# Expert weights streamed through a six-slot ring, moved in half matrices instead of whole ones

## The reference, cut to what matters

```python
N_EXPERTS, EXPERT_HIDDEN, D = 32, 512, 1024     # w_gate, w_up: [32, 1024, 512]; w_down: [32, 512, 1024]

def expert_block(args):
    xblk, e = args
    hid = jax.nn.silu(xblk @ w_gate[e]) * (xblk @ w_up[e])
    return hid @ w_down[e]
```

## Time and profile before

| | us |
|---|---|
| median of 3 runs (2041.07 to 2042.13) | 2041.3 |
| the profiled execution | 2040.8 |
| its span in the profile | 2039.0 |

### The profile page before, as it was taken

How to read it: one execution, slowest core, us unless ns; L and a number is a source line. 1 busy time by engine, 2 the same in 40 slices (tenths; PEclk the granted TensorE clock), 3 DMA queues, 4 the chain that set the end, 5 groups by cost and what they waited for, 6 DMA issues and landing times.

```text
span 2039.0 us, 25122 instructions
## 1 busy us (share of the span) xinstructions
PE 1973.0 (97%) x10310; PEld 1335.8 (66%) x10310; DVE 582.1 (29%) x1351; ACT 424.1 (21%) x961; POOL 12.9 (1%) x34
## 2 busy tenths in 40 slices
PE   8999999999999999998999999999998999999998
PEld 7798888957988888666455445445885455545544
DVE  3277450422555603422111011102233011101111
ACT  2440000322301101322221222122102222122212
POOL 1000000000001000000000000000000000000000
PEclk9998999989999999989999999999999999999999
DMA  9645576432357753213999999999544999999995
GB/s 334 199 170 218 236 305 247 166 111 84 137 233 285 306 220 132 83 42 123 400 429 429 427 429 429 428 429 428 208 148 157 400 430 427 429 428 428 428 429 226
DMA packets 51580, 591.24 MB, mean 290 GB/s; under 512 B 6305, under 2 KB 14761, under 8 KB 15794
## 3 DMA queue, kind: packets, MB, share of 16 engines
q1 hardware_dynamic: 51218, 588.09, 71.0%
q10 hardware_dynamic: 288, 2.10, 0.3%
HBM read 584.69 MB, written 1.05 MB: 287 GB/s over the span
## 4 chain that ended last, share of the span: by engine, by line
PE 70%; DMA 24%; DVE 4%; issue 1%; SPq 0%; ACT 0%; DVEq 0%
PE ps L436 24%; DMA ring<-in_w_up 22%; PE ps L1077 15%; PE ps L668 7%; PE ps L1167 4%; PE ps L1059 2%; PE ps L1065 2%; PE ps L711 2%; PE ps L495 2%; DVE work L1690 1%; DMA ring<-in_w_ada 1%; PE ps L583 1%; PE ps L462 1%; PE ps L511 1%; PE ps L526 1%
## 5 line engine op out<-in xcount | busy, mean ns | idle before, releaser
L1077 PE MATMUL ps<-ring,work 128*64 128x512 f32 x2048 | 450.3, 593 | 12.7 <-DMA ring<-in_w_up 12.2
L436 PE MATMUL ps<-h,ring 128*128 128x256 f32 x2064 | 457.1, 383 | 3.0 <-DVE h L1952 2.2
L436 PEld LDWEIGHTS ps<-h,ring 128*128 128x128 f32 x2064 | 394.0, 192 | 58.8 <-issue 4.0
L1077 PEld LDWEIGHTS ps<-ring,work 128*64 128x64 f32 x2048 | 151.2, 137 | 305.1 <-issue 290.4
L1349 ACT ACTIVATE work<-ps 128x512 f32<-128x512 f32 (+1 forms) x186 | 95.7, 519 | 715.0 <-PE ps L436 302.0
L1167 PE MATMUL ps<-ring,work 128*64 128x512 f32 x1024 | 226.8, 595 | 1.6 <-DVE work L2150 1.6
L1349 ACT ACTIVATE work<-ps,ada,scale_g 128x128 f32<-128x128 f32 x256 | 96.2, 456 | 411.3 <-PE ps L1059 411.3
L2141 DVE TENSOR_TENSOR work<-ps,work 128x512 f32<-128x512 f32 x32 | 22.1, 692 | 551.9 <-ACT work L1349 551.9
L1167 PEld LDWEIGHTS ps<-ring,work 128*64 128x64 f32 x1024 | 70.6, 137 | 133.6 <-issue 128.0
L668 PE MATMUL ps<-work,ring 128*128 128x256 f32 (+1 forms) x704 | 150.0, 376 | 3.9 <-DVE work L1867 3.9
L668 PEld LDWEIGHTS ps<-work,ring 128*128 128x128 f32 x704 | 131.3, 192 | 22.0 <-DVE work L1867 4.6
(11 more groups left out here) (295 smaller groups left out, 1282.2 us busy)
## 6 DMA issues: line engine op xcount, KB each, us to landing
ring<-in_w_gate SPq DMA_DIRECT2D x64, 2048.0 KB, 15.0
ring<-in_w_up SPq DMA_DIRECT2D x64, 2048.0 KB, 17.3
ring<-in_w_down SPq DMA_DIRECT2D x64, 2048.0 KB, 12.2
ring<-in_w_ada SPq DMA_DIRECT2D x24, 2048.0 KB, 8.5
ring<-in_w_ff_gate SPq DMA_DIRECT2D x10, 2048.0 KB, 14.8
ring<-in_w_ff_up SPq DMA_DIRECT2D x10, 2048.0 KB, 12.8
ring<-in_w_ff_down SPq DMA_DIRECT2D x8, 2048.0 KB, 10.9
ring<-in_ml_w_in SPq DMA_DIRECT2D x6, 2048.0 KB, 10.7
```

The lines of the kernel that those rows point to most:

```text
L436: last = mm(ps[:, b, 0:T], w[:, k, m * P:(m + 1) * P], rhs[:, k, :], start=(k == 0), stop=(k == nk - 1))
L1077: last = mm(ps[e * CAP:(e + 1) * CAP, j, :], xg[:, k, e * CAP:(e + 1) * CAP], w[e][:, k, :], start=(k == 0), stop=(k == KT - 1))
```

## The change

Each expert matrix is loaded by two DMAs of 1 MiB, each the first or the second half of every partition's row. In `gathered_tokens` the halves have signals of their own: `gate_half` and `up_half` after step k = 3, beside `gate_full` and `up_full`; for down the existing `half_done` and `down_done`. SP waits for a half's signal and loads that half of both experts of the next pair. PE still waits for both halves of both matrices before it begins with a kind. The down matrix is stored with its column half outermost, so that half a row is what one value of c reads. The wait values go from 16 to 32 per expert load (`landed`). The branch for crowded experts (`all_tokens`) waits as before and loads two halves each time. To have semaphores for the new signals, some that are never needed apart are merged (`lru_decay` and `lru_root` into `lru_powers`, `f_abs` and `gate_m` into `gate_args`, `z_sq` and `z_root` into `z_stats`, `all_squares` into `row_full`); each waiter waits for the same instructions as before.

```diff
@@ PE, gathered_tokens and its helpers
-                    gate_step(k, [matrices(first, e)[2][0] for e in range(2)])
+                    last = gate_step(k, [matrices(first, e)[2][0] for e in range(2)], last_k=KT // 2 - 1)
+                last.then_inc(e_["gate_half"], 1)
...
-                            pe.wait_ge(slot_loaded[slots[j]], 16 * i + loads[j])
+                            pe.wait_ge(slot_loaded[slots[j]], 32 * i + loads[j])
...
                             last = gate_step(k, [pair_of[e][2][j] for e in range(2)], j)
+                            if k == KT // 2 - 1:
+                                last.then_inc(e_["up_half" if j else "gate_half"], 1)
                         last.then_inc(e_[done], 1)
...
-                                          pair_of[e][2][2][:, k, c * 512:(c + 1) * 512],
+                                          pair_of[e][2][2][:, c, k, :],
@@ SP, load_experts
-                order = [(0, 0), (0, 1), (1, 0), (1, 1), (2, 0), (2, 1)]
+                order = [(w, e) for w in range(3) for e in range(2)]
+
+                def load_half(w, e, part, expert):
+
+                    slot = (first + 2 * w + e) % RING
+                    at = slice(part * SLOT // 2, (part + 1) * SLOT // 2)
+                    sp.dma_start(ring[:, slot, at], weights[w][l, expert][:, at]).then_inc(slot_loaded[slot], 16)
+
                 for j, (w, e) in enumerate(order):
-                    n = first + j
-                    sp.wait_ge(*released[n - RING])
-                    sp.dma_start(ring[:, n % RING, :], weights[w][l, e]).then_inc(slot_loaded[n % RING], 16)
+                    sp.wait_ge(*released[first + j - RING])
+                    for part in range(2):
+                        load_half(w, e, part, e)
...
-                    with sp.Fori(0, NEXP // 2 - 1) as i:
-                        for j, (w, e) in enumerate(order):
-
-                            s_, per, at = done(w, e)
-                            sp.wait_ge(s_, per * i + at)
-                            slot = (first + j) % RING
-                            sp.dma_start(ring[:, slot, :], weights[w][l, 2 * i + (2 + e)]).then_inc(
-                                slot_loaded[slot], 16)
...
+                def pairs_of_gathered_tokens():
+
+                    freed = (("gate_half", "gate_full"), ("up_half", "up_full"), ("half_done", "down_done"))
+                    with sp.Fori(0, NEXP // 2 - 1) as i:
+                        for w in range(3):
+                            for part in range(2):
+                                sp.wait_ge(e_[freed[w][part]], i + 1)
+                                for e in range(2):
+                                    load_half(w, e, part, 2 * i + (2 + e))
+                    next_layer(lambda w, e: (e_[freed[w][1]], 1, 1))
@@ layout of the down matrices in DRAM
-    w = g["w_down_2"].reshape(2, NEXP, HTL, P, D)
-    arrays["w_down"] = np.ascontiguousarray(w.transpose(0, 1, 3, 2, 4)).reshape(2, NEXP, P, SLOT)
+    w = g["w_down_2"].reshape(2, NEXP, HTL, P, 2, D // 2)
+    arrays["w_down"] = np.ascontiguousarray(w.transpose(0, 1, 3, 4, 2, 5)).reshape(2, NEXP, P, SLOT)
```

More of the change, by code:

```diff
@@ L368, in build, with landed @@
         seam_rows = (HTL + 2 * HTL, KT - 1 + 2, KT - 3 + 2 * 3)
+        def landed(n):
+            experts = lambda m: any(0 <= m - first < 3 * NEXP for first in moe_first)
+            return sum(32 if experts(m) else 16 for m in range(n % RING, n + 1, RING))
         def conditions(l, c):
@@ L415, in next_chunk @@
                     state["chunk"] += 1
-                pe.wait_ge(slot_loaded[n % RING], 16 * (n // RING + 1))
+                pe.wait_ge(slot_loaded[n % RING], landed(n))
                 _, nk, cols = chunks[n]
@@ L1071, in matrices, with gate_step @@
                 slots = [j % RING for j in n]
-                return slots, [16 * (j // RING + 1) for j in n], [
-                    ring[:, slots[j], :].rearrange("p (k c) -> p k c", k=KT if j < 2 else HTL) for j in range(3)]
-            def gate_step(k, w, j=0):
+                return slots, [landed(j) for j in n], [
+                    ring[:, slots[0], :].rearrange("p (k c) -> p k c", k=KT),
+                    ring[:, slots[1], :].rearrange("p (k c) -> p k c", k=KT),
+                    ring[:, slots[2], :].rearrange("p (h k c) -> p h k c", h=2, k=HTL)]
+            def gate_step(k, w, j=0, last_k=KT - 1):
                 for e in range(2):
                     last = mm(ps[e * CAP:(e + 1) * CAP, j, :], xg[:, k, e * CAP:(e + 1) * CAP], w[e][:, k, :],
-                              start=(k == 0), stop=(k == KT - 1))
+                              start=(k == 0), stop=(k == last_k), skip_group_check=True)
                 return last
@@ L1161, in down @@
                     for slots, loads, _ in pair_of:
-                        pe.wait_ge(slot_loaded[slots[2]], 16 * i + loads[2])
+                        pe.wait_ge(slot_loaded[slots[2]], 32 * i + loads[2])
                     for c in range(2):
@@ L1278, in rest, with pairs_of_all_tokens, done @@
                             put(n)
+                def pairs_of_all_tokens():
+                    def done(w, e):
+                        return ((e_["gate_full"], 8, 4 * e + 4), (e_["up_full"], 8, 4 * e + 4), (e_["down_done"], 2, e + 1))[w]
+                    with sp.Fori(0, NEXP // 2 - 1) as i:
+                        for w, e in order:
+                            s_, per, at = done(w, e)
+                            sp.wait_ge(s_, per * i + at)
+                            for part in range(2):
+                                load_half(w, e, part, 2 * i + (2 + e))
+                    next_layer(done)
+                def pairs_of_gathered_tokens():
+                    freed = (("gate_half", "gate_full"), ("up_half", "up_full"), ("half_done", "down_done"))
+                    with sp.Fori(0, NEXP // 2 - 1) as i:
+                        for w in range(3):
+                            for part in range(2):
+                                sp.wait_ge(e_[freed[w][part]], i + 1)
+                                for e in range(2):
+                                    load_half(w, e, part, 2 * i + (2 + e))
+                    next_layer(lambda w, e: (e_[freed[w][1]], 1, 1))
                 with sp.If(most > CAP):
-                    rest(lambda w, e: ((e_["gate_full"], 8, 4 * e + 4), (e_["up_full"], 8, 4 * e + 4),
-                                       (e_["down_done"], 2, e + 1))[w])
+                    pairs_of_all_tokens()
                 with sp.Else():
-                    rest(lambda w, e: (e_[("gate_full", "up_full", "down_done")[w]], 1, 1))
+                    pairs_of_gathered_tokens()
             load(1)
@@ L1432, in _ @@
             for j in range(HTL):
-                turn.give(A(rate[:, j, :], th[:, j, :], ACT.Exp, scale=lamt[:, 24 + j:25 + j]), S["lru_decay"])
-            turn.own(S["lru_decay"])
+                turn.give(A(rate[:, j, :], th[:, j, :], ACT.Exp, scale=lamt[:, 24 + j:25 + j]), S["lru_powers"])
+            turn.own(S["lru_powers"])
             for j in range(HTL):
@@ L1511, in _ @@
             value_out(0, 0)
-            turn.take(S["f_abs"])
+            turn.take(S["gate_args"])
             turn.give(A(ghead[:, 2, :], ghead[:, 2, :], ACT.Exp, scale=-1.0), achain)
@@ L1517, in _ @@
             value_out(1, 0)
-            turn.take(S["gate_m"])
+            turn.take(S["gate_args"])
             turn.give(A(ghead[:, 3, :], ghead[:, 3, :], ACT.Exp, scale=-1.0), S["gate_expm"])
@@ L1795, in _ @@
             step(V.tensor_tensor(bx[:], bx[:], xr[:], ALU.mult))
-            turn.take(S["lru_decay"], HTL)
-            turn.take(S["lru_root"])
+            turn.take(S["lru_powers"], HTL)
+            turn.take(S["lru_powers"])
             step(stt(den_a, rate, 1.0, den_a, ALU.add, ALU.mult))
@@ L1826, in ada_make @@
                 if half == 0:
-                    dve.wait_ge(slot_loaded[n % RING], 16 * (n // RING + 1))
+                    dve.wait_ge(slot_loaded[n % RING], landed(n))
                 ws = range(conditions(l, c))
@@ L2000, in _ @@
                 if i == 3:
-                    turn.take(S["z_root"])
-                    turn.take(S["z_sq"], TT)
+                    turn.take(S["z_stats"])
+                    turn.take(S["z_stats"], TT)
                     step(V.reciprocal(small[:, 8:10], small[:, 6:8]))
```

38 lines of the change are left out of this document (19 added, 19 removed).

## The result

| | before | after |
|---|---|---|
| median of 20 runs each, us | 2041.17 (2037.93 to 2046.56) | 2046.51 (2040.01 to 2053.76) |
| ratio of after to before, 95% interval | | 1.0023 (1.0014 to 1.0033) |
| span of the profiled execution, us | 2039.0 | 2041.3 |
| its time, us | 2040.8 | 2043.1 |

The change made the kernel 5.3 us slower by the medians, 0.26% (the ratio in the table is 1.0023). In the profiles much of the difference between two executions arises ahead of the expert stages: the first gate product comes at 951.96 us in after, at 954.41 before, and anywhere from 951.50 to 958.00 in the other kernels of this document, which ahead of it differ at most in pair 0's loads and the merged semaphores.

The account below looks back on a forecast made before the run. The DMA queue's rate was taken to bound the late expert pairs. Per layer, -3.51 (early down) + 6.25 (rows) + 0.39 (DMAs) = +3.13 us; two layers +6.3, so the median becomes 2047.6 us, range 2036.5 to 2053.5.

Parts of the forecast that it names:

- What bounds the kernel: Mixture layers, late pairs: paced by what the DMA queue can move, 428.6 GB/s, not by when a slot comes free.
- The knot's spacing: Repeating waits from the fifth pair (in_w_up DMA, PE's up products, next DMA): starts 29.36 us apart, forecast to become 29.84.
- the rival of depth: Late pairs: a longer queue makes the engines move more, so PE sets the pace; about -17 us, 2024.8; chance 0.03.
- The price of a row: Expert loads: each extra row costs an engine 9.3 ns; 672 rows more make 6.25 us a layer (3.96 to 8.47).
- The price of twice the DMAs: Expert loads: signals of 84 more DMAs to the load that counts, 0 to 0.78 us a layer, 0.39 taken.
- The early half of down: Pair 1's first down half is issued 3.51 us earlier, into an empty queue: -3.51 us a layer, -7.0 in all.
- one sign named for being wrong: Queue ahead of pair 1's down: an idle stretch as long as now would show the prediction wrong.
- Gate and up halves bring nothing: Other 14 pairs: gate and up halves released earlier only lengthen a queue that is never empty: 0.
- The rest at 0: PE's matmuls, down's new column order, signals added to matmuls and merged semaphores: 0; nothing waits for anything new.
- the pair where PE begins to wait: Mixture layers: PE begins to wait at the sixth or seventh pair instead of the fifth.
- Sum of a layer: Each mixture layer: -3.51 + 6.25 + 0.39 = +3.13 us; two layers +6.3.
- The rival of free rows: Expert loads: rows of 8 KiB cost nothing more, leaving -7.0 us: 2034.3, or up to 2037.2; chance 0.13.

Follow-up runs that it names:

- the late and the early kernel: Late: the changed kernel, each half loaded only when the kernel before would have loaded the whole matrix, +12.2 us against before; early: the changed kernel itself, +5.3 us.
- The run with pair 1 alone: Kernel before, with only pair 1's down matrices loaded in halves, the first behind half_done; all other pairs whole: -1.4 us, ratio 0.9982 to 1.0001.

## Why the prediction was right

The forecast was 2047.6, the median is 2046.5, inside the range, and in the direction forecast. By its steps:

- *What bounds the kernel.* Right. The knot's spacing is a pair's bytes at the queue's rate: every kernel with shorter rows throughout moved it (29.53, 29.69, 29.82, 30.72), and the three that load later pairs whole and only issued some loads earlier kept it (29.36, 29.37, 29.36). With more loads waiting in it the queue was not faster (29.82 in after, 29.83 with the same halves released late), so the rival of depth falls as well.
- *The price of a row,* 9.3 ns with ends at 5.9 and 12.6, taken from 1 KiB rows. Measured 9.5 ns at 8 KiB and 9.4 at 4 KiB. The four readings from the narrow chunks scattered by a factor of two, and their mean lay well; the spread of the range was honest and the mean partly luck. The estimate from the 408.7 GB/s that the Trainium skill gives ("DMA: Bandwidth & Descriptors", section "iDMA fabric — 4 AXI ports for 8 engines, asymmetric across TPBs"), 9.9 ns, is borne out too: the run with 4 KiB rows moved 410 GB/s.
- *The price of twice the DMAs,* 0.39 us a layer: put too high. Twelve DMAs and six with the same rows have spacings 0.01 and 0.02 us apart, 0.1 to 0.3 us a layer, and after, with twelve, has the spacing of six.
- *The early half of down,* -3.51 us: -3.57 and -3.52 between the late and the early kernel. Right in size and in time (978.88 is 26.9 us behind pair 0's gate; the 981.4 forecast was 27.0 behind its own). But one sign named for being wrong, an idle stretch ahead of down as long as now, came nearly true: 2.0 and 1.9 us instead of 2.4 and 2.6. The prediction had itself put the end of gate and up ahead of the down half's issue, so its two statements on this stretch did not fit together; the gain hangs on the time of issue, not on a filled hole.
- *Gate and up halves bring nothing.* Borne out for the stream as a whole: alone they lose 3.9 to 4.4 us a stage, near the 4.3 of their rows' price.
- *The rest at 0, the pair where PE begins to wait.* Pair 7 in both layers (pair 5 and pair 6 before), forecast the sixth or seventh.
- Sum of a layer: forecast +3.13; +2.0 and +2.8 in the two profiled stages. The first has the wider miss in part because its last up load of before took 22.31 us instead of 21.76; why, stays open.

The rival of free rows, which the rule of the Trainium skill's "Perfetto Trace Analysis", section "DMA Optimizations", would have made the outcome (only loads under 2 KB are called costly), falls with the late halves: at 8 KiB, on a queue without idle time, halving cost 12 us. The other sentence of that section, that splitting may let some loads start sooner, names its condition, idle DMA engines, and the runs show both sides of it.

One step was incomplete, and no forecast number shows it. The prediction credited the 3.51 us to pair 1's down alone and gave the other pairs' early downs no work to do. The run with pair 1 alone kept 1 to 2 us of it a stage. The gain was kept in the changed kernel because the later downs were early as well: at the pace of PE pair 2's whole down would have come 3.51 us later than its half did, for a queue that by the reckoning from issue to issue has only 0.77 us to spare. The first forecast made from that gap, -7.1 us for one early pair, failed by 5.7 us.

## What to carry to other kernels

On a queue that never runs dry an earlier load is worth nothing and a shorter row costs its fixed time, so split only where a window shows the queue empty, and stop splitting as soon as its backlog covers the wait. A lead given to one load lasts only if every later load that would otherwise find the queue empty is moved as well: compare, pair by pair, the time that the queue's work runs out with the time of the next issue. When an idle stretch is no longer where it was, look in the windows around it before calling it filled: here it had moved with the stream in one kernel and to the next pair in another.

## What the runs showed that was not expected

- The price of a DMA row is a straight line at sizes where one might take it for nothing: 9.5 ns a row and engine at 8 KiB (the bytes of such a row take 306 ns, worked out from 428.6 GB/s over 16 engines), 9.4 at 4 KiB; 429, 422 and 410 GB/s with rows of 16, 8 and 4 KiB at a full queue. Whether two DMAs of 1 MiB or one of 2 MiB carry the rows made a difference of 0.01 to 0.02 us in 29.8.
- The spread between executions of one kernel is larger than the effect: 2040.0 to 2053.8 us in 20 runs of after. It goes with the mean granted clock of TensorE, 0.985 and 0.984 in the shortest (2040.2 and 2040.0), 0.979 in the longest. In the expert stages the granted clock is 1.00 in before and after, but for a few microseconds in pair 0 behind a pause of PE (0.83 in the mean from 970 to 980 us in both, with 0.50, the lower of its two levels, over some three of them); the spacing of the up loads is the same to 0.02 us in both layers, so lengths measured inside a stage told kernels apart that single executions could not.
